# Instructions merged per head pair in three attention stages, stick-breaking in sixteen rounds, full-width value products in the NSA softmax

## What is computed

```python
# NSA: with 8 blocks and top-k 8 every block is chosen: two causal softmaxes
# over 512 keys (chosen blocks, window) and one over 31 compressed keys
o = g[..., 0:1] * o_cmp + g[..., 1:2] * o_slc + g[..., 2:3] * o_win
# stick-breaking
z = q @ k.T * scale
log_fail = where(before, log_sigmoid(-z), 0.0)
later = cumsum(log_fail, reverse=True) - log_fail
a = where(before, exp(log_sigmoid(z) + later), 0.0);  o = a @ v
# band: keys of the own and the earlier chunks of 64
prob = softmax(where(valid, q @ k.T * scale + bias, NEG_INF));  o = prob @ v
```

## Time and profile before

| | us |
|---|---|
| three runs | 1578.88, 1579.07, 1581.48 (median 1579.07) |
| profiled execution | 1579.92 |
| its span | 1578.2 |
| TensorE busy, granted clock | 1488.9 (94%), 0.982 |
| VectorE / ScalarE / GpSimd busy | 837.6 / 686.4 / 205.5 |

### The profile page before, as it was taken

The page is one execution under the profiler, slowest core; times in us unless marked ns, Lnnn a source line. Parts: engine busy times, 40 slices in busy tenths (PEclk is TensorE's granted clock), DMA queues, the critical chain, the costliest instruction groups (busy, mean ns, idle before and its releaser), DMA issues.

```text
span 1578.2 us, 22125 instructions
## 1 busy us (share of the span) xinstructions
PE 1488.9 (94%) x8593; PEld 1252.4 (79%) x8593; DVE 837.6 (53%) x1444; ACT 686.4 (43%) x1305; POOL 205.5 (13%) x309
## 2 busy tenths in 40 slices
PE   4999998999989999999989998988999999999997
PEld 2788866678988888888888886668988888888986
DVE  5767645577464444432275345875654444422364
ACT  4555535377443222322353235886542232222453
POOL 0000000144310000000130003653300000000211
PEclk9999999799999999999999999999999999999999
DMA  9533340002213333333403331003033333333321
GB/s 375 211 94 101 120 153 9 1 2 68 94 55 102 96 93 95 102 96 93 147 1 107 95 92 54 5 24 108 1 94 93 96 103 93 93 111 97 114 81 54
DMA packets 40531, 143.06 MB, mean 91 GB/s; under 512 B 4464, under 2 KB 6528, under 8 KB 39808
## 3 DMA queue, kind: packets, MB, share of 16 engines
q1 hardware_dynamic: 38240, 129.55, 25.8%
q0 software_dynamic: 1632, 11.52, 2.0%
q10 hardware_dynamic: 576, 0.85, 0.2%
HBM read 139.81 MB, written 2.10 MB: 90 GB/s over the span
## 4 chain that ended last, share of the span: by engine, by line
PE 81%; DVE 8%; ACT 5%; issue 3%; POOL 1%; DMA 1%; DVEq 0%; SPq 0%; POOLq 0%; ACTq 0%
PE B L277 24%; PE B L278 23%; PE B L279 23%; PE B L1646 3%; ACT T L560 2%; PE B L1730 1%; PE B L1528 1%; PE B L1866 1%; POOL T L480 1%; PE B L1625 1%; DVE WADA L1069 1%; DMA X<-in_x 1%; DVE WL L1023 1%; DVE KEPT_L L1021 1%; DVE X L1034 1%
## 5 line engine op out<-in xcount | busy, mean ns | idle before, releaser
L277 PE MATMUL B<-UH,WH 128*128 128x512 f32 (+1 forms) x1120 | 420.7, 376 | 17.1 <-DVE UL L1078 6.3
L278 PE MATMUL B<-UL,WH 128*128 128x512 f32 (+1 forms) x1120 | 417.0, 372 | 0.0
L279 PE MATMUL B<-UH,WL 128*128 128x512 f32 (+1 forms) x1120 | 416.9, 372 | 0.0
L277 PEld LDWEIGHTS B<-UH,WH 128*128 128x128 f32 x1120 | 212.1, 189 | 57.7 <-DVE UL L1041 7.6
L560 ACT ACTIVATE WH<-RAW 128x1024 fp32r<-128x1024 f32 x178 | 186.6, 1051 | 137.2 <-DMA RAW<-in_stream 117.0
L278 PEld LDWEIGHTS B<-UL,WH 128*128 128x128 f32 x1120 | 212.3, 190 | 36.3
L279 PEld LDWEIGHTS B<-UH,WL 128*128 128x128 f32 x1120 | 212.2, 189 | 36.4
L1023 DVE TENSOR_TENSOR WL<-RAW,WH 128x1024 fp32r<-128x1024 f32 x98 | 121.9, 1246 | 165.6 <-ACT WH L560 165.4
L560 ACT ACTIVATE T<-B 128x256 f32<-128x256 f32 (+3 forms) x207 | 96.0, 466 | 126.1 <-PE B L279 64.5
L1323 DVE TENSOR_TENSOR WL<-RAW,WH 128x1024 fp32r<-128x1024 f32 x80 | 98.1, 1226 | 76.7 <-ACT WH L560 74.0
L560 ACT ACTIVATE T<-T 128x512 f32<-128x512 f32 (+3 forms) x131 | 68.6, 525 | 134.2 <-DVE T L1327 119.2
(11 more groups left out here) (340 smaller groups left out, 2928.9 us busy)
## 6 DMA issues: line engine op xcount, KB each, us to landing
RAW<-in_stream SPq DMA_DIRECT2D x202, 512.0 KB, 3.6
WADA<-in_w_ada SPq DMA_DIRECT2D x4, 2048.0 KB, 18.8
RAW<-in_stream SPq DMA_DIRECT2D x16, 384.0 KB, 3.2
WADA<-in_w_ada SPq DMA_DIRECT2D x4, 1024.0 KB, 18.4
W<-in_w POOLq DMA_DIRECT2D x2, 2048.0 KB, 11.3
X<-in_x SPq DMA_DIRECT2D x2, 1024.0 KB, 10.5
DECAY<-in_decay POOLq DMA_DIRECT2D x1, 2048.0 KB, 8.1
X<-in_x POOLq DMA_DIRECT2D x2, 1024.0 KB, 8.4
```

Of the source, the lines that this page charges most:

```text
L277: nc.tensor.matmul(out, lh, rh, start=start, stop=False, **kw)
L278: nc.tensor.matmul(out, lh, rl, start=False, stop=False, **kw)
L279: return nc.tensor.matmul(out, ll, rh, start=False, stop=stop, **kw)
```

## The change

PSUM is allocated in four pairs of banks (`TWO`; `B[n]` are their halves), and one instruction may cover both heads of a pair (two runs of L columns, 512 apart).
- softmax stages: one hi, one lo, one inverse per pair; in NSA one maximum too (the band's stays one per unit). Counters are raised by two; an instruction for both heads waits for both.
- stick-breaking: sixteen rounds (head pair, kj) instead of 32 units, each VectorE, ScalarE and GpSimd step one instruction for both heads. The rings hold two rounds, the banks three. The order within a step is new: VectorE soft of the round before, clamp of this one, weights_lo of three rounds before, soft_lo of the round before; ScalarE hi, exp, weights of two rounds before, log. The filler of the steady state goes.
- NSA value products: `VN` holds the high and low part of V side by side, so 128 stationary columns give V high in rows 0 to 63 and V low in rows 64 to 127 of the bank; two products (with the low and the high weights) for each block instead of three. A new VectorE step `at_sum` adds the upper half to T[10] and T[11] after `at_x`, in iterations 12, 20, 28 and 36, ahead of that iteration's maximum; the next `nsa_first` and the gate multiply wait for it. `BD` gets 128 columns, the upper 64 zero.

```diff
-        VNH, VNL = hb("VNH", 88, [P, 4, 256], F32R), hb("VNL", 92, [P, 4, 256], F32R)
+        VN = hb("VN", 88, [P, 4, 4, 2, HD], F32R)
...
-        BD = hb("BD", 57, [P, 2, 4, HD])
+        BD = hb("BD", 57, [P, 2, 4, P])
...
+        TWO = [nc.alloc_psum_tensor(f"TWO{n}", [P, 2, SEQ], F32) for n in range(4)]
+        B = [TWO[n // 2][:, n % 2, :] for n in range(8)]
...
+        S_PAIR, PT_PAIR = TWO[1:3], TWO[3]
+        Z_RING, SP_RING, P_RING = ([at(f"T{n}T{n + 1}", OFF_T + n * 2 * KB, [P, 2, SEQ]) for n in ring] for ring in ((0, 8), (2, 6), (4, 10)))
...
+        SB_EARLY, SB_ALONE = 2, 18
+        def sb_banks(r):
+            return TWO[0] if r == 0 else TWO[1 + (r - 1) % 3]
+        def sb_unit(r):
+            return r // 4, 3 - r % 4
+        def sb_len(r):
+            return SEQ - P * sb_unit(r)[1]
+        def sb_soft_tiles(r):
+            p, kj = sb_unit(r)
...
+                return SP0H[:, :, :], SP0L[:, :, :]
+            o, w = {3: 2 * (p % 2), 2: 4, 1: 8}[kj] * P, 2 * (SEQ - P * kj)
+            return tuple(part[:, o:o + w].rearrange("p (s n) -> p s n", s=2) for part in (SPH, SPL))
...
-            o = slice(kind * P + g * HD, kind * P + (g + 1) * HD)
...
-                    "v": lambda b: (VNH[:, b, o], VNL[:, b, o])}
+                    "both": lambda b: VN[:, b, 2 * kind + g, :, :]}
...
+            def drop_later(tiles, done):
+                done.mark(nc.gpsimd.affine_select(out=tiles[:, :, 0:P], in_=tiles[:, :, 0:P], pattern=[[0, 2], [1, P]],
...
+            def sb_later(r):
+                p, kj = sb_unit(r)
+                wait(pool, E["sb_sp"], r + 1)
+                drop_later(SP_RING[r % 2], E["sb_spm"])
+                wait(pool, E["sb_spm"], r + 1)
+                wait(pool, E["sb_zz"], 4 * (p - (kj == 3)))
+                E["sb_sph"].mark(nc.gpsimd.tensor_copy(sb_soft_tiles(r)[0], SP_RING[r % 2][:, :, 0:sb_len(r)]))
+            def sb_later_weights(r):
+                wait(pool, E["sb_p"], r + 1)
+                drop_later(P_RING[r % 2], E["sb_pm"])
+            for r in range(SB_EARLY):
+                sb_later(r)
+            for r in range(SB_EARLY):
+                sb_later_weights(r)
...
+            for r in range(SB_EARLY + 1, 18):
+                if r - 1 < 16:
+                    sb_later(r - 1)
+                if r - 2 >= SB_EARLY:
+                    sb_later_weights(r - 2)
...
+            wait(pool, E["sb_zz"], 16)
...
+                        u, at = 2 * (m - 3), slice(2 * (m - 3) % 4, 2 * (m - 3) % 4 + 2)
+                        L = units[u]["L"]
+                        wait(act, tag["tr"], u + 2)
+                        wait(act, tag["pv"], u - 2)
+                        tag["hi"].mark(f(AH2[:, at, 0:L], PT_PAIR[:, :, 0:L], ACT.Copy), 2)
...
+            sb_e = Event("sb_e")
+            def sb_exp(r):
+                z = Z_RING[r % 2][:, :, 0:sb_len(r)]
+                wait(act, E["sb_m"], r + 1)
+                sb_e.mark(f(z, z, ACT.Exp))
+            def sb_log(r):
+                z = Z_RING[r % 2][:, :, 0:sb_len(r)]
+                wait(act, sb_e, r + 1)
...
+            def sb_weights(r):
+                L = sb_len(r)
+                wait(act, E["sb_zz"], r + 1)
+                wait(act, E["sb_lo"], r - 1)
+                E["sb_p"].mark(f(P_RING[r % 2][:, :, 0:L], sb_banks(r)[:, :, 0:L], ACT.Exp))
+            def sb_weights_hi(r):
+                L = sb_len(r)
+                wait(act, E["sb_pm"], r + 1)
+                wait(act, E["sb_pv"], r - 1)
+                E["sb_hi"].mark(f(AH[:, 2 * (r % 2):2 * (r % 2) + 2, 0:L], P_RING[r % 2][:, :, 0:L], ACT.Copy))
...
+            def sb_heads_out(p):
+                for s in range(2):
+                    head_out(SBN, 2 * p + s, YA, E["sb_pv"], 4 * p + 4)
+            def stick_breaking(r):
+                if r >= 8 and r % 4 == 0:
+                    sb_heads_out(r // 4 - 2)
+                if 0 <= r - 3 < 16:
+                    sb_weights_hi(r - 3)
+                if r < 16:
+                    sb_exp(r)
+                if SB_EARLY <= r - 2 < 16:
+                    sb_weights(r - 2)
+                if r < 16:
+                    sb_log(r)
+            for r in range(SB_EARLY, SB_ALONE):
+                stick_breaking(r)
...
+                if m < 2:
...
+                if m == 2:
+                    sb_heads_out(3)
...
+                    if m < N and units[2 * m]["bias"] is None:
+                        u = 2 * m
+                        wait(dve, tag["s"], u + 2)
+                        tag["max"].mark(v.tensor_reduce(NMAX[:, u % 8:u % 8 + 2], S_PAIR[m % 2][:, :, 0:units[u]["L"]], AX.X,
+                                                        ALU.max, negate=True), 2)
+                    elif m < N:
...
+                            wait(dve, tag["tr"], u - 7)
+                            dve.wait_ge(bias_here if units[u]["h"] < 4 else bias_rest, 16)
+                            ins = v.tensor_tensor_reduce(S_RING[u % 8][:, 0:L], S[:, 0:L], units[u]["bias"], -1.0, 3.0e38,
+                                                         ALU.add, ALU.min, top)
...
+                        u, at = 2 * (m - 3), slice(2 * (m - 3) % 4, 2 * (m - 3) % 4 + 2)
+                        L = units[u]["L"]
+                        wait(dve, tag["hi"], u + 2)
+                        tag["lo"].mark(tt(AL2[:, at, 0:L], PT_PAIR[:, :, 0:L], AH2[:, at, 0:L], ALU.subtract), 2)
...
+                        u = 2 * (m - 1)
+                        wait(dve, tag["exp"], u + 2)
+                        tag["rec"].mark(v.reciprocal(RECS[:, u % 8:u % 8 + 2], SUMS[:, u % 8:u % 8 + 2]), 2)
...
+                if m >= 12 and (m - 12) % 8 == 0:
+                    j = (m - 12) // 8
+                    for s in range(2):
+                        rows = pair_rows(j)
+                        wait(dve, at_x, 2 * j + s + 1)
+                        at_sum.mark(tt(T[10 + s][rows, :], B[s][HD:P, :], T[10 + s][rows, :], ALU.add))
...
+                        wait(dve, at_sum, 4 * (m // 36) + 3 + s)
...
+            def sb_clamp(r):
+                L = sb_len(r)
+                wait(dve, E["sb_z"], r + 1)
+                wait(dve, E["sb_sp"], r - 1)
+                E["sb_m"].mark(ts(Z_RING[r % 2][:, :, 0:L], sb_banks(r)[:, :, 0:L], 40.0, None, ALU.min))
+            def sb_soft(r):
+                L = sb_len(r)
+                wait(dve, E["sb_l"], r + 1)
+                wait(dve, E["sb_spl"], r - 1)
+                E["sb_sp"].mark(tt(SP_RING[r % 2][:, :, 0:L], sb_banks(r)[:, :, 0:L], Z_RING[r % 2][:, :, 0:L], ALU.max))
+            def sb_soft_lo(r):
+                hi, lo = sb_soft_tiles(r)
+                wait(dve, E["sb_sph"], r + 1)
+                E["sb_spl"].mark(tt(lo, SP_RING[r % 2][:, :, 0:sb_len(r)], hi, ALU.subtract))
+            def sb_weights_lo(r):
+                L, at = sb_len(r), slice(2 * (r % 2), 2 * (r % 2) + 2)
+                wait(dve, E["sb_hi"], r + 1)
+                E["sb_lo"].mark(tt(AL[:, at, 0:L], P_RING[r % 2][:, :, 0:L], AH[:, at, 0:L], ALU.subtract))
...
+                    for step in (sb_clamp, sb_soft, sb_soft_lo):
+                        for r in range(SB_EARLY):
+                            step(r)
...
+            def stick_breaking(r):
+                if SB_EARLY <= r - 1 < 16:
+                    sb_soft(r - 1)
+                if r < 16:
+                    sb_clamp(r)
+                if 0 <= r - 3 < 16:
+                    sb_weights_lo(r - 3)
+                if SB_EARLY <= r - 1 < 16:
+                    sb_soft_lo(r - 1)
+            for r in range(SB_EARLY, SB_ALONE):
+                stick_breaking(r)
...
+                                if units is NSA_UNITS:
+                                    at = slice(b * P, (b + 1) * P)
+                                    mat(B[s][:, i * P:(i + 1) * P], x["both"](b), AL2[:, u % 4, at],
+                                        start=False, stop=False, skip_group_check=True)
+                                    ins = mat(B[s][:, i * P:(i + 1) * P], x["both"](b), AH2[:, u % 4, at],
+                                              start=False, stop=b == i, skip_group_check=True)
+                                    continue
...
+                    wait(pe, at_sum, 2 * (m // 8 - 1) + s + 1)
+                    mat(B[s][:, :], BD[:, s, m // 8, :], PTC[:, s, :], start=True, stop=False, skip_group_check=True)
...
+            def sb_scores(r):
+                p, kj = sb_unit(r)
+                cols, L = slice(kj * P, (kj + 1) * P), SEQ - P * kj
+                done = score_pair([sb_banks(r)[:, s, 0:L] for s in range(2)],
...
+                E["sb_z"].mark(done[1])
+            def sb_later_sums(r):
+                kj = sb_unit(r)[1]
...
+                wait(pe, E["sb_spl"], r + 1)
+                for s in range(2):
+                    for tile in range(kj, 4):
+                        w = SEQ - P * tile
+                        for n, part in enumerate(sb_soft_tiles(r - (tile - kj))):
```

(30 more changed lines are left out.)

199 lines of the change are left out of this document (18 added, 181 removed).

## The result

The changed kernel takes 1621.7 us (median of four executions, 1612.25 to 1629.03) against 1580.28 for the kernel before on the same chip, a ratio of 1.0254, 95% interval 1.0197 to 1.0311. The prediction was 1604, range 1585 to 1619: slower is right, by +41.4 us instead of +24.7. The profiled execution is one of the longer ones, 1627.67 us with a span of 1625.9, and the spans differ by 47.7.

A forecast was written before the change was run, and what follows sets the result against it. It took NSA as paced by TensorE, stick-breaking and band as rings of latencies in which every engine waits. NSA 15.1, stick-breaking 7.3 and band 2.3 give +24.7 us on the median of 1579.07: 1604 us, range 1585 to 1619.

The forecast's parts named there:

- Value products: NSA: two wide products 110 ns apart replace three at 60 ns, 220 instead of 180 ns a block; +5.6 us.
- Rival (b): Wide NSA products 60 ns apart, or alternatively stick-breaking as dense as now (14.7 us a cycle); about 1593 us; chance 0.16.
- Lo of a 512-wide pair: NSA: TensorE's next transposes wait 1.25 us for merged lo, before 0.33; +0.92 a group, four groups, +3.7 us.
- Lo of a 384-wide pair: NSA: the same wait for merged lo at two pairs of a group, 0.05 us each; +0.4 us in all.
- Head change: NSA: the next head's first product waits for the copy and at_sum; +0.9 us, three times, +2.7 us.
- NSA by groups: NSA's terms per group of eight pairs, 21.28 us before, 24 us or more forecast; whole stage +15.1 us.
- the two f32 products: NSA head change: 1.0 us of products, taken as cover for VectorE's maximum and lo queued behind the waiting sum.
- the end of the stage: NSA's drain, where nothing covers the ring: the weight part TensorE awaits at 391.75 moves by +2.4 us.
- Stick-breaking and band: Stick-breaking: cycle 17.6 against 15.78 us, +6.3, and last chain +1, together 7.3; band: hi, lo, reciprocal merged, +2.3 us.
- Two of the four steps: Stick-breaking cycle: the 128-column step forecast at 4.34 us and the 256-column step at 4.76 us.
- "+1" for it: End of stick-breaking: about ten handovers, each now waiting for both heads, about 0.1 us each; +1 us.
- Rival (a): Stick-breaking: TensorE's clock falls, at half of 2.4 GHz 2.6 us more per cycle; +9, 1613 us; chance 0.25.

The follow-up runs named there:

- e4_after_fill: The changed kernel with filler products that compute nothing ahead of the scores, in TensorE's waits in NSA and band; 1613.82 us, ratio 1.0217.
- e12: Kernel before with merged softmax instructions and sixteen stick-breaking rounds, narrow value products, plus filler products in the band's waits; 1604.08 us, ratio 1.0146.
- e2_merges: Kernel before with the softmax merges alone (hi, lo, reciprocal in both stages, max in NSA), narrow value products; 1595.35 us, ratio 1.0097.
- e5: The changed kernel with the stick-breaking stage of before: wide value products and merged softmax instructions together; 1613.2 us, ratio 1.0188.
- e9: Kernel before with wide value products, and in NSA the first head's lo made more than once, nothing merged; 1603.51 us, ratio 1.0145.

## Why the prediction was right and wrong

- **Value products**: right. 110 ns from start to start, 16 in 1.91 us, a group of 22.4 to 23.3 us with them alone. The gap of 81 ns that the Trainium skill gives ("TensorE: Matmul & The Clock Gate", Back-to-back issue gap) would have made them a gain and does not hold for this form here. Rival (b) falls: the products are not 60 ns apart, and a cycle of stick-breaking is 17.20 us and not 14.7.
- **Lo of a 512-wide pair**: right, 1.24 to 1.29 us of reported wait (1.25 predicted). **Lo of a 384-wide pair**: 0.15 in the changed kernel, 0.05 predicted.
- **Head change**: 0.55 and 0.69 us of wait, 0.9 predicted. Right in kind.
- **NSA by groups**: the terms give +3.5 a group. The first two groups of the changed kernel cost +3.3 and +3.5. With the clock up (e4_after_fill) the third costs +4.9, the rest of the stage +6.8 against 4.2. So the sum is good where its picture holds. It left out that VectorE's gate multiply and split queue ahead of lo in the third group (waits of 0.56 and 0.35: the two f32 products were not the cover it took them for), and had the end of the stage too small.
- **Stick-breaking and band**: cycle 17.20 against 17.6 predicted. Two of the four steps do not add up as written (4.34 and 4.76, where their terms give 4.44 and 4.64); the errors cancel. Alone the parts cost 7.1 (7.3 predicted) and 2.8 (2.3), and that this agrees is partly luck: both figures have 1.5 us less for the fillers at full clock. The band stage costs +4.3 with the merges alone and +4.5 with the rounds alone, most of the latter in the tail of stick-breaking, where one wait is 2.05 us: "+1" for it was too small.
- **Sum of the parts**: 24.7 predicted, 32.0 measured part by part. Of the 7.3, 3.6 are NSA (18.7 against 15.1). The rest is the band and the tail: 0.3 in the stretches as measured, 3 more that the fillers at full clock hid in both profiled executions, which agrees with these being 1.6 us faster than their medians.
- **The step that failed**: the sum gave TensorE's clock no term in NSA and in the band. Rival (a) had the mechanism but looked for it in stick-breaking, where the clock held (0.97 from 1000 to 1060; two dips of 3.4 us in the stage, as before the change). It read NSA as it was before the change, "with hardly a hole", although its own sum put holes of 1.25 and 0.9 us there; what these do to the clock was not asked. By the medians, the 41.4 are 24.7 predicted, 7.3 for parts dearer than summed, and 9.4 for the clock in NSA. The profiled execution is 6 us above the median and shows more: NSA took 29.7-19.2 = 10.5 us more than with fillers; the stages behind it 18.0-11.1 = 6.9 more than e12's, which has them without falls but without wide products too. So its 47.7 are 24.7 predicted, 4.1 (NSA, 19.2-15.1) and 1.5 (behind it, 11.1-9.6) undersized, and 10.5 and 6.9 mostly of clock.
- **The range** ended at 1619, since it knew one place for the fall. The changed kernel spreads over 17 us (1612.25 at a mean clock of 0.976, 1629.03 at 0.961), the kernel before over 5: how often the clock falls seems to differ from execution to execution.

Open: why wide products or merges alone leave the clock up. In the slice from 360 to 370 us e2_merges is 8.43 us busy at a clock of 1.00, the changed kernel 8.40 at 0.85; busy time does not tell them apart. Whether the added waits of the third group are what makes the fall come there was not tested: no run takes the gate multiply and the split out of it. Which execution without a profile had the fall is read from its mean clock alone.

## What to carry to other kernels

Merging two heads' instructions saves 0.07 us of an engine that was not the limit, and makes the next engine wait for the second head. Where the limiting engine waits for the buffer that the first head frees, this costs it more than is saved: here 1.24 us of wait for each such 512-wide pair. Where an engine's instructions wait in a fixed order, look also for the iteration in which others are added ahead of the one that the limit waits for: the third group here. When a sum puts new idle time on TensorE, price two cases, with its clock up and with it halved in what follows, and let the range reach to the second. Idle stretches on TensorE that precede work on the path can be filled with products into a bank about to be overwritten: here that gave 11 us to the kernel before and 8 to the changed one.

## What was not expected of the hardware

- At half clock TensorE reads as busy 100% (370 to 390 us): the fuller slice is the slower one.
- The first two groups have waits of 1.24 us each and stay at full clock (310 to 360); the fall came in the third, which has more of them. In some executions it seems not to come at all: 1603 or 1614 us for e5, 1598 or 1609 to 1614 for e9.
- The clock stayed at 0.50 for 23.9 us (366.9 to 390.8) although the engine had no hole in that time.
